# Adding transfers in DRAM: 128 rows as the outer dimension, and the three groups of pairs interleaved

## What is computed

```python
def first_block(x, ..., w_gate, w_up, w_down, ln_post_ffn):
        ...
        x = x + rms_norm(mix, ln_post_mix[l])
        h = rms_norm(x, ln_pre_ffn[l])
        f = (jax.nn.silu(h @ w_gate[l]) * (h @ w_up[l])) @ w_down[l]
        x = x + rms_norm(f, ln_post_ffn[l])
    return x

def conv_gated_mlp(h, w_up, conv_w, conv_b, w_down):
    ...
    gate, val = jnp.split(c, 2, axis=-1)
    return (jax.nn.silu(gate) * val) @ w_down
```

## Time and profile before

| what | value |
|---|---|
| time, median of 3 runs | 1381.69 us (1379.53 to 1382.72) |
| the profiled execution's own time | 1381.75 us |
| its span in the trace | 1379.8 us |
| PE busy | 1278.3 us (93%) |
| DVE, ACT, POOL busy | 957.3, 729.0, 516.0 us |
| mean rate of all DMA | 126 GB/s |

### The profile page before, as it was taken

One profiled execution on the slowest core, in us unless ns is written; L12 is line 12 of the kernel. 1 busy time (PEld: TensorE's weight loads), 2 busy tenths in 40 slices (PEclk: granted clock), 3 DMA queues, 4 the chain that ended last, 5 costly groups with the idle time before them and its releaser, 6 DMA issues.

```text
span 1379.8 us, 22055 instructions
## 1 busy us (share of the span) xinstructions
PE 1278.3 (93%) x7684; PEld 1158.3 (84%) x7684; DVE 957.3 (69%) x1732; ACT 729.0 (53%) x1437; POOL 516.0 (37%) x578
## 2 busy tenths in 40 slices
PE   8989558999999999999969667999999999999998
PEld 7978457899999998888968657998989999877887
DVE  5767356589988878974535446855798777779754
ACT  4655344455555555655635445853545555556452
POOL 6626348135655610126739547631021322200000
PEclk9999789999999999999989988999999999999999
DMA  7568654223323248625457646323222332384321
GB/s 236 185 145 171 112 119 96 92 92 123 122 92 121 91 153 260 175 78 183 125 136 142 118 87 116 92 93 97 90 93 78 120 106 76 107 297 138 122 92 61
DMA packets 165575, 173.61 MB, mean 126 GB/s; under 512 B 45388, under 2 KB 131611, under 8 KB 165490
## 3 DMA queue, kind: packets, MB, share of 16 engines
q1 hardware_dynamic: 129600, 145.15, 33.1%
q0 software_dynamic: 35888, 27.34, 11.7%
q10 hardware_dynamic: 2, 0.00, 0.0%
HBM read 170.22 MB, written 39.85 MB: 152 GB/s over the span
## 4 chain that ended last, share of the span: by engine, by line
PE 67%; DMA 11%; DVE 7%; POOL 7%; issue 5%; ACT 2%; SPq 0%; ACTq 0%; DVEq 0%; POOLq 0%
PE ps L2832 12%; PE ps L2833 12%; PE ps L2834 12%; DMA down_sums<-in_w_down_dram 6%; PE ps L2951 3%; PE ps L2958 3%; PE ps L2953 3%; PE ps L3084 3%; PE ps L3088 3%; PE ps L3086 3%; DVE w_lo L2381 2%; DMA tables<-in_rel_table_dram 2%; PE ps L3128 2%; PE ps L3129 2%; PE ps L3130 2%
## 5 line engine op out<-in xcount | busy, mean ns | idle before, releaser
L2832 PE MATMUL ps<-h_hi,w_hi 128*128 128x256 f32 (+1 forms) x748 | 238.7, 319 | 0.0
L2833 PE MATMUL ps<-h_lo,w_hi 128*128 128x256 f32 (+1 forms) x748 | 237.8, 318 | 0.0
L2834 PE MATMUL ps<-h_hi,w_lo 128*128 128x256 f32 (+1 forms) x748 | 237.4, 317 | 0.0
L2951 PE MATMUL ps<-w_hi,h_hi 128*128 128x384 f32 (+2 forms) x512 | 167.7, 337 | 0.0
L2953 PE MATMUL ps<-w_hi,h_lo 128*128 128x384 f32 (+2 forms) x512 | 162.7, 327 | 0.0
L2834 PEld LDWEIGHTS ps<-h_hi,w_lo 128*128 128x128 f32 x748 | 142.8, 191 | 9.7
L2832 PEld LDWEIGHTS ps<-h_hi,w_hi 128*128 128x128 f32 x748 | 142.9, 191 | 9.2 <-DVE h_lo L2128 0.3
L2833 PEld LDWEIGHTS ps<-h_lo,w_hi 128*128 128x128 f32 x748 | 142.9, 191 | 8.6
L1271 POOL TENSOR_TENSOR w_lo<-w_raw,w_hi 128x384 fp32r<-128x384 f32 (+2 forms) x114 | 126.9, 1249 | 23.0 <-ACT w_hi L1512 22.9
L2958 PE MATMUL ps<-w_lo,h_hi 128*128 128x384 f32 (+2 forms) x512 | 105.6, 326 | 18.5 <-POOL w_lo L1271 17.7
L2958 PEld LDWEIGHTS ps<-w_lo,h_hi 128*128 128x128 f32 x512 | 86.9, 194 | 20.9 <-POOL w_lo L1271 19.9
(11 more groups left out here) (327 smaller groups left out, 3391.6 us busy)
## 6 DMA issues: line engine op xcount, KB each, us to landing
w_raw<-in_w_up_dram SPq DMA_DIRECT2D x25, 1024.0 KB, 5.3
w_raw<-in_w_in_dram SPq DMA_DIRECT2D x69, 256.0 KB, 4.4
w_raw<-in_w_gate_dram SPq DMA_DIRECT2D x11, 1024.0 KB, 5.3
down_sums<-in_w_down_dram SPq DMA_DIRECT2D x18, 512.0 KB, 5.4
down_sums<-in_w_down_dram SPq DMA_DIRECT2D x36, 256.0 KB, 6.3
down_sums<-in_w_down_dram POOLq DMA_DIRECT2D x12, 768.0 KB, 28.9
down_sums<-down_sums POOLq DMA_DIRECT2D x12, 768.0 KB, 8.9
w_raw<-in_w_out_dram SPq DMA_DIRECT2D x8, 1024.0 KB, 5.3
```

The source lines that it names most:

```text
L2832: pe.matmul(out_, s_hi, m_hi, start=first and n == 0, stop=False, skip_group_check=True)
L2833: pe.matmul(out_, s_hi, m_lo, start=False, stop=False, skip_group_check=True)
L2834: mm = pe.matmul(out_, s_lo, m_hi, start=False, stop=last and n == len(pairs) - 1, skip_group_check=True)
L2951: pe.matmul(bank, h_hi[:, kb0 + i, tok], hi[:, i, :], start=half == 0 and i == 0, stop=False, skip_group_check=True)
```

## The change

The twelve adding transfers of a mixer stay at the same unit counts, with the same bytes and the same sums. Two things differ. Both sides of each transfer are written as [128 rows, 3 pairs, 512] in place of [3 pairs, 128 rows, 512]. And the order is no longer group by group (T3, T1, T2, T4), but that of ADD_ORDER. Since T1 of a group now comes before T3, the wait for `sums_begun` moves to T1.

```diff
+ADD_ORDER = ((0, "T1"), (0, "T3"), (0, "T2"), (1, "T1"), (0, "T4"), (1, "T3"),
+             (1, "T2"), (2, "T1"), (1, "T4"), (2, "T3"), (2, "T2"), (2, "T4"))
 ADD_AFTER = ((9, 12, 15, 18, 20, 23, 25, 27, 29, 32, 35, 38), (8, 11, 14, 17, 20, 23, 26, 29, 32, 35, 38, 41))
...
                         if normed_units in ADD_AFTER[mx.b]:
-                            n = ADD_AFTER[mx.b].index(normed_units)
-                            sums_added(mx.b, n // 4, ("T3", "T1", "T2", "T4")[n % 4])
+                            sums_added(mx.b, *ADD_ORDER[ADD_AFTER[mx.b].index(normed_units)])
...
-                to = lambda n: down_sums[d][group(g), :, n, :]
-                from_w = lambda quarter: weight_quarter(d, group(g), quarter)
+                to = lambda n: down_sums[d][group(g), :, n, :].rearrange("j p n -> p j n")
+                from_w = lambda quarter: weight_quarter(d, group(g), quarter).rearrange("j p n -> p j n")
                 chain, ready = sums_chain[g], sums_ready[g]
                 if name == "T3":
-                    pool.wait_ge(sums_begun[g], 48 * (STRASSEN // GROUPS) * (d + 1))
                     pool.dma_start(to(SUM_T3), from_w("B22"), accum_op=ALU.add).then_inc(ready, 16)
                 elif name == "T1":
+                    pool.wait_ge(sums_begun[g], 48 * (STRASSEN // GROUPS) * (d + 1))
                     pool.dma_start(to(SUM_T1), from_w("B11"), accum_op=ALU.add).then_inc(chain, 16)
```

## The result

The changed kernel takes 1271.72 us (median of 4 runs, 1271.42 to 1273.01), the kernel before 1381.46 us in the runs beside it: a ratio of 0.9209, 95% interval 0.9193 to 0.9224. That is 109.7 us less.

What follows compares the result with a forecast made beforehand. PE was held up by POOL, which stood 128.5 us behind slow T1 transfers on about three DMA engines. Idle 82.4 plus clock 21.5 is 103.9, less 17 new costs, 87 us off 1381.75: 1295 us, range 1280 to 1330.

Steps and rivals of the forecast that it cites:

- Three engines: T1 and T3 run on about three DMA engines; with 128 rows outside, on 16, landing in some 10 us, not 28.9.
- The issues on POOL: T2 and T4 no longer fold, so issuing on POOL rises from 1011 to 2073 ns, some 3.6 us a mixer.
- The distances: In the new order nearly all distances between dependent adding transfers exceed 10 us, so nearly all 128.5 us of POOL's waits go.
- The starting values of the third group: First mixer: their wait comes two units earlier at T1, should just be met; 0 to 8 us allowed once.
- What PE gets back: In both mixers' adding stretches, PE regains 82.4 us of idle time and 21.5 us of lowered clock, together 103.9 us.
- What comes in its place: New costs in the mixers: left-over POOL waits 5 us, POOL's crowding 5, fuller DMA engines 7.
- Sum 17: Total of the new costs charged in the mixers, 17 us, taken off the 103.9 us gain to leave 87.
- (a): DMA engines become the bound, rows 1 MiB apart being slower: 15 us for each mixer, 1325 us; chance 0.17.
- (b): Only the order works; T1 and T3 still need 28.9 us, T2 waits 30 us in all: 1314 us; chance 0.09.
- (c): POOL becomes the bound of the second mixer, not fillable past 85%: 1305 us; chance 0.08.
- (d): Nothing gained: all twelve transfers run on three engines at 28.9 us, 116 us of waits: 1372 us; chance 0.02.
- (e): Slower: rows 1 MiB apart fill the DMA engines, 13 us more in each mixer: 1407 us; chance 0.03.

Runs made afterwards that it cites:

- the two added loads: Changed kernel plus, ahead of each of the 24 adding transfers, a plain 768 KB copy (1306.26 us) or some 2.5 us of POOL arithmetic (1307.07 us).
- The two kernels with six slow transfers: Changed kernel with three pairs outside again for T1 only (1347.76 us) and for T3 only (1352.64 us).
- the kernel without waits: Order-only kernel (new order, three pairs outside) with T2 and T4 left out, so POOL waits for no adding transfer: 1322.34 us.

## Why the prediction was right or wrong

**Three engines.** Right. T1 and T3 land after 9.2 us where some 10 were taken, and the kernel with 6 and 3 as outermost dimensions gave 17.6 and 28.4 us where 18 and 29 were expected. The rule of the Trainium skill, page "DMA: Bandwidth & Descriptors", section "Why a DMA increments its semaphore by 16 and not by 1", gives 3, 6 and 16 engines for these forms; the landing times agree.

**The issues on POOL.** Of the right kind, mis-sized. T2 and T4 went from some 1.0 us to 1254 and 1286 ns in the median, not to 2 us, and T1 and T3 fell from some 2.0 to 1.28 us. The long issue belonged to the few engines, not to three dimensions: in the kernel with cut forms it is 1.45 us for 6 and 2.00 us for 3. The third dimension costs T2 and T4 at most 0.3 us.

**The distances.** Right: one of the twelve T2 and T4 still waits, for 1.1 us, at a distance of three units. The starting values of the third group came in time.

**What PE gets back.** Right in kind, some 6 us too small. Of idle time 82.4 us were predicted and 86.3 came; for the clock 21.5 us were predicted and 23.8 of busy time came. Together that is 110.1 us against 103.9. The kernel without adding transfers gained 112.6. Of the 6.2 us of idle time that were held back as not to be had, the 4.0 us around POOL's pooling steps did not stay whole: in the changed kernel PE loses 1.45 us where they begin.

```profile
150.00:160.00 10.00, 9.79 (x55) 8.21 (x55) 8.18 (x24) 8.94 (x20) 7.73 (x8) 1.00 0.72 133
160.00:170.00 10.00, 8.76 (x50) 7.05 (x49) 9.56 (x25) 7.79 (x18) 9.34 (x13) 1.00 0.67 166
```

**What comes in its place.** This is the step that failed: "Sum 17", of 5 for left-over waits, 5 for POOL's crowding and 7 for the DMA engines. The kernel without adding transfers is 2.9 us faster than the changed one, so all three together cost about 2.9 us. Busy shares of 0.89 were turned into costs with no row that tied a cost to them. For the DMA engines a row even spoke against it: a share of 1.05 over 6 us with PE busy for all 6. It was used against rival (a) and not against the prediction's own charge. For POOL the one row as dense spoke for a cost (18.15 of 20 us, PE busy for 16.00). The 23 us between forecast and result are the 17 us of this charge and the 6 us by which the gain was too small. The charge was not baseless, as the two added loads show: 35 us each. So the cost is near nothing at the present load and large somewhat above it, and not in proportion; where it begins was not measured.

**The rivals.** (a) did not come: the transfers from w_down landed after 9.2 us with rows 1 MiB apart, T2 and T4 of before after 8.9. The slower rates for row pitches of 512 KiB and 2 MiB, which the Trainium skill gives in the section "Latency and other measured facts" of the same page for copies of 16 KiB rows on other queues, don't show in this pattern. A share of 1.05 is no sign that PE must wait. One argument against (a) was misread: no row shows four such transfers under way with PE at full rate, since in 158 to 164 us one T2 runs beside a load, at a clock of 0.75. (b) was wrong in size, 1314 against 1362.41 us measured for the order alone: it counted each transfer by its own landing and left out what a transfer on three engines does to those behind it. (c), (d) and (e) did not come. Of the chances, half of (d) as same makes 0.96 faster and 0.01 same, not 0.95 and 0.02.

**A cause that was too narrow.** The prediction put the whole loss on POOL's waits for T1. The runs show a second effect of the same transfers: they hold up others, in POOL's own queue and in SP's, and cost 51 us when nobody waits for them at all. That this happens on their few engines is argued and not shown. Before the change, too, SP needed 9.74 us to issue the three loads at 81.92 us:

```profile
81.92 9.74 SPq L1160 DMA_DIRECT2D w_raw<-in_w_in_dram  x3
```

The two effects probably overlap there, since SP's loads wait for POOL anyway. The forecast for the change did not suffer, since the rows remove both; that for the order alone did.

## What to carry to other kernels

Look at the DMA share while a slow transfer runs alone: 0.21 of 16 engines with an outer dimension of 3 names the fault, and writing the rows outside mends it, at no cost that shows here. Mend the transfer before moving it: an order that hides its landing (19 us here) leaves in place what it does to the loads beside it, where the mended form brought 103 us. And don't charge for a busy engine until a row shows a stretch that is as busy and slower; try it by adding load.

## What the runs showed of the hardware

Written with three pairs outside, the queue's 9227 packets of 2 KB took 178 ns each in the median, and with 128 rows outside 178 ns too. The packets are not slower; fewer engines carry them. An estimate from their mean, 204 ns before: a transfer has 384 of them, 78 us of one engine's work, or 26 us for three engines, 13 for six and 5 for sixteen. Landing took 28.9, 17.6 and 9.2 us.

A transfer on few engines also has more packets. Each of the twelve from w_down had 1664 more with three pairs outside: (35888 - 15920) / 12 = 1664 = 13 x 128, which fits one for each of the 13 engines left out and each of the 128 rows that a used engine carries. By this rule, written down before the run, the kernel with 6 and 3 had to have 15920 + 6 x 10 x 64 + 6 x 13 x 128 = 29744 packets, and it had. The two kernels with six slow transfers have 25904 = 15920 + 6 x 1664. Each of these packets has 8 bytes in the trace. They go with the longer issue on POOL: 1.28 us with none, 1.45 us with 640, 2.0 us with 1664. On which engines they lie the trace doesn't say.

Slow transfers in one queue go with slow issuing in another: SP needed up to 10.2 us to issue three loads in the kernel without waits, and up to 16.7 us with T1 slow, where the changed kernel needed 1.5 to 2.7. It doesn't take few engines. With the added copies, 128 rows outside, it happened once in the first mixer as well:

```profile
109.39 15.18 SPq L1164 DMA_DIRECT2D w_raw<-in_w_in_dram  x3
```
